# First two products from x times gain, the norm applied to their results, first weight chunks loaded between the quarters of x

## What is computed

```python
def first_block(x, ...):
    for i in range(DEPTH):
        h = _rmsnorm(x, attn_norm[i])
        proj = jnp.matmul(h, w_in[i])
        q_a, c_kv, q_idx, k_idx, w_idx, qkv_b, gate_a, gate_b = _split_cols(proj)
        c_kv = _rmsnorm(c_kv, kv_norm[i])
        ...
        x = x + jnp.matmul(merged, w_out[i])
        ...
```

## Time and profile before

| | us |
|---|---|
| median of 3 runs | 2364.31 |
| lowest, highest | 2362.16, 2365.21 |
| span of the profiled execution | 2358.2 |
| TensorE busy in it | 2261.0 (96%) |
| VectorE, ScalarE, GpSimd busy | 919.8, 772.5, 773.1 |

### The profile page before, as it was taken

The page is one execution under the profiler, slowest core; times in us unless marked ns, Lnnn a source line. Parts: engine busy times, 40 slices in busy tenths (PEclk is TensorE's granted clock), DMA queues, the critical chain, the costliest instruction groups (busy, mean ns, idle before and its releaser), DMA issues.

```text
span 2358.2 us, 30460 instructions
## 1 busy us (share of the span) xinstructions
PE 2261.0 (96%) x12044; PEld 1719.9 (73%) x12044; DVE 919.8 (39%) x1370; ACT 772.5 (33%) x1154; POOL 773.1 (33%) x414
## 2 busy tenths in 40 slices
PE   7999999979999899999999999999999999999997
PEld 5776667633333379668899999888877686888885
DVE  2586453331111463433660362353000524721722
ACT  4335555211111433653421222333322424222222
POOL 3341226211111134204244444334433044544541
PEclk9899999979999999999999999999999999999999
DMA  4421113668999322102223232222322022333330
GB/s 160 144 83 61 45 46 116 245 240 352 353 350 383 115 86 90 45 9 63 65 95 92 89 89 90 90 91 91 96 72 80 1 90 79 98 93 97 98 98 36
DMA packets 69360, 278.03 MB, mean 118 GB/s; under 512 B 13016, under 2 KB 13144, under 8 KB 56960
## 3 DMA queue, kind: packets, MB, share of 16 engines
q1 hardware_dynamic: 59408, 259.61, 31.9%
q0 software_dynamic: 9552, 16.51, 2.0%
q10 hardware_dynamic: 288, 0.34, 0.1%
HBM read 323.58 MB, written 19.42 MB: 145 GB/s over the span
## 4 chain that ended last, share of the span: by engine, by line
PE 87%; DVE 4%; issue 4%; POOL 2%; ACT 2%; DMA 0%; DVEq 0%; POOLq 0%; SPq 0%; ACTq 0%
PE ps L871 19%; PE ps L890 17%; PE ps L1334 7%; PE ps L1093 5%; PE ps L522 4%; PE ps L1136 4%; PE ps L1356 4%; POOL weights_low L2705 2%; PE ps L1295 2%; PE ps L1120 2%; PE ps L641 2%; PE ps L1197 2%; PE ps L732 1%; PE ps L852 1%; PE ps L624 1%
## 5 line engine op out<-in xcount | busy, mean ns | idle before, releaser
L2705 POOL TENSOR_TENSOR weights_low<-weights,parts 128x1024 fp32r<-128x1024 f32 x250 | 632.3, 2534 | 1064.9 <-ACT parts L1884 1064.9
L871 PE MATMUL ps<-parts 128*128 128x264 f32 x2384 | 447.2, 283 | 0.0
L890 PE MATMUL ps<-parts 128*128 128x512 f32 x1344 | 416.1, 390 | 1.3 <-ACT area L1406 1.0
L1884 ACT ACTIVATE parts<-weights 128x1024 fp32r<-128x1024 f32 x257 | 269.1, 1054 | 400.7 <-PE ps L871 133.8
L871 PEld LDWEIGHTS ps<-parts 128*128 128x128 f32 x2384 | 372.9, 188 | 0.0
L871 PE MATMUL ps<-parts,weights_low 128*128 128x264 f32 x1120 | 317.3, 283 | 0.0
L890 PEld LDWEIGHTS ps<-parts 128*128 128x128 f32 x1344 | 252.3, 188 | 56.0 <-issue 1.2
L890 PE MATMUL ps<-parts,weights_low 128*128 128x512 f32 x672 | 262.5, 391 | 0.0
L871 PEld LDWEIGHTS ps<-parts,weights_low 128*128 128x128 f32 x1120 | 211.1, 188 | 0.0
L1334 PE MATMUL ps<-area,normed 128*64 128x512 f32 x752 | 171.5, 597 | 1.6 <-DVE normed L2393 1.6
L2178 DVE TENSOR_TENSOR parts<-normed,parts 128x528 f32 (+1 forms) x64 | 160.5, 2508 | 9.6 <-DVE normed L2177 2.0
(11 more groups left out here) (459 smaller groups left out, 3600.0 us busy)
## 6 DMA issues: line engine op xcount, KB each, us to landing
weights<-in_weights SPq DMA_DIRECT2D x283, 512.0 KB, 3.5
area<-in_experts SPq DMA_DIRECT2D x141, 1024.0 KB
area<-pair_rows SPq DMA_DIRECT2D x4, 1024.0 KB, 7.9
bias_scratch<-bias_vector POOLq DMA_DIRECT2D x1, 2560.0 KB, 18.3
residual<-in_x SPq DMA_DIRECT2D x4, 512.0 KB, 6.4
area<-bias_scratch POOLq DMA_DIRECT2D x1, 2048.0 KB, 9.0
token_rows<-area SPq DMA_DIRECT2D x1, 2048.0 KB, 8.2
out_tiles<-residual SPq DMA_DIRECT2D x4, 512.0 KB, 2.8
```

What stands on the lines that cost most here:

```text
L871: ins = mm(ps[:, b + h, 0:HALF], wt[:, k], x[m * DT + k][:, HALF * h:HALF * h + HALF], start=m == k == j == 0, stop=m == chunks - 1 and k ...
L890: ins = mm(ps[:, b], wt[:, k], x[:, m * DT + k, first:first + SEQ], start=m == k == j == 0, stop=m == chunks - 1 and k == DT - 1 and j == 2)
L1884: fn(high_slot(n, place), RING[:, n % SLOTS], ACT.Copy).then_inc(S["w_hi"], 1)
L2705: g.tensor_tensor(RING_LOW[:, n % SLOTS], RING[:, n % SLOTS], high_slot(n, place), ALU.subtract).then_inc(S["w_lo"], 1)
```

## The change

SyncE issues one quarter of x, chunks 0 and 1, the other three quarters, then chunks 2 to 7. VectorE multiplies each tile of x by its gain alone (`XG`), and TensorE takes the first two products from `XG` and chunks 0 and 1; VectorE multiplies the two results by `R` later. The partition sum of the norm stands behind 13 of those 16 products in TensorE's order. The first two split chunks go through `first_pair`, which waits for a tile of `x_hi` or `x_lo` at a time. Four places instead of two hold high parts of weights, so `high` runs two chunks further ahead, and `high(2)` and `high(3)` stand before and behind the inverse deviation. Squares go to a place of their own (`SQ_FIRST`). The rest of the diff is counts and names.

```diff
-        IN_FIRST = [[part(20480 + D * j, D) for j in range(2)], None]
+        IN_FIRST = [[part(at, D) for at in (20480, 21504, 22528, 32256)], None]
+        XG, SQ_FIRST = area(7168, DT, SEQ), area(23552, DT, SEQ)
...
-            for j in range(4):
+            def load_x(j):
                 sp.dma_start(XA[:, 2 * j:2 * j + 2], a["x"][:, 2 * j:2 * j + 2]).then_inc(x_in[j], 16)
+
+            load_x(0)
...
             for c in range(SLOTS):
                 load(c, slice(c, c + 1))
+                if c == 1:
+                    for j in (1, 2, 3):
+                        load_x(j)
...
                 pe.wait_ge(S["consts"], 32)
-                rms_sum(HA[:, DT - 1])
-
-                hn = lambda k: HA[:, k]
                 begin_stage("act_evac")
+                banks, pair = [bank(), bank()], [take(), take()]
+                for c, k in [(c, k) for k in range(DT - 2) for c in range(2)] + [(c, k) for c in range(2) for k in (DT - 2, DT - 1)]:
+                    if c == 0:
+                        pe.wait_ge(S["norm_out"], w.next("norm_out"))
+                    if (c, k) == (0, DT - 1):
+                        rms_sum(SQ_FIRST[:, DT - 1])
+                    ins = mm(ps[:, banks[c]], pair[c][:, k], XG[:, k], start=k == 0, stop=k == DT - 1)
+                    if (c, k) in ((0, 0), (1, DT - 2)):
+                        begun(ins)
+                    if k == DT - 1:
+                        ins.then_inc(S["tile_done"], 1)
+                first_pair(HH, HL, IN_FIRST, [(0, 0, SEQ)], banks=[bank(), bank()])
                 for n in range(2):
-                    linear(hn, take(), fresh=n == 0)
-                pe.wait_ge(S["x_hi"], w.next("x_hi", DT))
-                pe.wait_ge(S["x_lo"], w.next("x_lo", DT))
-                for n in range(4):
                     linear_split(HH, HL, IN_FIRST)
+                pe.wait_ge(S["norm_out"], w.next("norm_out", DT))
...
-                    fn(HA[:, t], XA[:, t], ACT.Square).then_inc(S["norm_sq"], 1)
+                    fn(SQ_FIRST[:, t], XA[:, t], ACT.Square).then_inc(S["norm_sq"], 1)
                 act.wait_ge(S["consts"], 32)
+                high(2, place=IN_FIRST, slots=-1)
                 inverse_deviation(SEQ, D, "eps1")
+                high(3, place=IN_FIRST, slots=-1)
...
-                for n in (2, 3):
+                for n in (4, 5):
                     high(n, place=IN_FIRST, slots=-1)
...
             def body():
+                dve.wait_ge(S["consts"], 32)
                 for n in range(DT):
-                    total(n, HA, SEQ, "norm_sq", n + 1)
-                dve.wait_ge(S["consts"], 32)
+                    if n % 2 == 0:
+                        dve.wait_ge(x_in[n // 2], 16)
+                    v.tensor_scalar(XG[:, n], XA[:, n], vec("attn_norm", n), None, ALU.mult).then_inc(S["norm_out"], 1)
+                    if n % 2:
+                        for m in (n - 1, n):
+                            total(m, SQ_FIRST, SEQ, "norm_sq", m + 1)
                 rms(8, SEQ, "attn_norm", lambda t: XA[:, t], lambda t: HA[:, t])
                 for t in range(DT):
                     dve.wait_ge(S["x_hi"], w.next("x_hi"))
                     v.tensor_tensor(HL[:, t], HA[:, t], HH[:, t], ALU.subtract).then_inc(S["x_lo"], 1)
+                dve.wait_ge(S["act_evac"], w.next("act_evac", 2))
+                for x in (CKV, KI):
+                    v.tensor_tensor(x, x, R[:, 0:SEQ], ALU.mult).then_inc(S["norm_out"], 1)
```

More of the change, by code:

```diff
@@ L331, in square @@
             return (HA if v < 2 else RK[:, :, B1])[:, 2 * i + v % 2]
[L333 to L336, removed]
+        names = """consts norm_sq norm_sum norm_sd norm_out act_ops dve_ops pool_ops
+            tile_done act_evac dve_evac chunk_begun rel_done rel_sb rel_used score_cut score_mask
+            bias_vec bias_dram bias_rows bias_rep small_in logits smax expd diag tr pt o_done o_evac             z_done soft sp sp_masked c_done a_raw a_masked merged
             route_done route_ev route_e rank_done table_in table_rows table iota_in gate_on sg
@@ L340, in build @@
             p_in meta_in out_done ln_cent ln_out c2_in c3_in hot_in bvec_out wr_in route_x lam_exp gelu_in gelu_th
-            gelu_done xq w_hi w_lo x_hi x_lo lru_t pad_zero lru_x lru_r lru_done hidden mla_ones q_ready k_rope k_ready m_rows m_in mla_s mla_p mla_o mla_om mla_d mla_dm mla_y mla_ym ret_s ret_used ret_o ret_y decay_in sum_part sq_pair hl_kept g_lo roped y_hi y_lo route_t route_c sq_added""".split()
+            gelu_done w_hi w_lo x_hi x_lo lru_t pad_zero lru_x lru_r lru_done mla_ones q_ready k_rope k_ready m_rows m_in mla_s mla_p mla_o mla_om mla_d mla_dm mla_y mla_ym ret_s ret_used ret_o ret_y decay_in sum_part sq_pair hl_kept g_lo roped y_hi y_lo route_t route_c sq_added""".split()
         S = {n: ctx.enter_context(nc.semaphore(n)) for n in names}
@@ L573, in body @@
                         pe.wait_ge(S["bias_dram"], w.next("bias_dram", 1))
+                        pe.wait_ge(S["norm_out"], w.next("norm_out", 2))
                     relevance(range(EACH * c, min(EACH * c + EACH, len(RELS))))
@@ L894, in linear_parts, with first_pair @@
                 ins.then_inc(S["tile_done"], 1)
-            def first_pair(high, low, place, cols):
-                banks = [2 * bank() for _ in range(2)]
+            def first_pair(high, low, place, cols, banks=None):
+                banks = banks or [2 * bank() for _ in range(2)]
                 pair = [take_parts(place) for _ in range(2)]
@@ L1431, in body @@
                     if n >= 2:
-                        high(n + 2, place=IN_FIRST, slots=-1)
+                        high(n + 4, place=IN_FIRST, slots=-1)
                 if w.counted("tile_done"):
@@ L1435, in body @@
                 w.count("tile_done")
+                act.wait_ge(S["norm_out"], w.next("norm_out", 2))
                 squares(1, lambda t: CKV, lambda t: R1)
@@ L1442, in body @@
                     evac(out, bank(n), scale=QK_SCALE if n < 8 else 1.0)
-                    high(n + 8, place=IN_FIRST, slots=-1)
+                    high(n + 10, place=IN_FIRST, slots=-1)
                     for m in range(EACH * n, min(EACH * n + EACH, len(RELS))):
@@ L1452, in body @@
                     fn(HL_KEPT[:, t], HL[:, t], ACT.Copy).then_inc(S["hl_kept"], 1)
-                for n in (20, 21):
-                    high(n, place=IN_FIRST)
                 for n in range(2):
@@ L2030, in body @@
                     chosen_keys(t)
-                dve.wait_ge(S["act_evac"], w.next("act_evac", 30))
+                dve.wait_ge(S["act_evac"], w.next("act_evac", 28))
                 w.count("tile_done", 30 - 6)
@@ L2656, in body @@
                     low(n, IN_PLE)
-                pool.wait_ge(S["norm_out"], w.next("norm_out", 33))
+                pool.wait_ge(S["norm_out"], w.next("norm_out", 43))
                 pool.dma_start(MASKW, a["causal"]).then_inc(S["c2_in"], 16)
```

1 line of the change is left out of this document (added).

## The result

| | before | after |
|---|---|---|
| median of 5 runs, us | 2362.82 (2362.16 to 2365.21) | 2374.09 (2368.73 to 2376.04) |
| ratio | | 1.0041, 95% interval 1.0029 to 1.0053 |
| profiled execution, span in us | 2358.2 | 2371.9 |
| mean granted clock of TensorE | 0.983 | 0.975 |

The forecast was a gain of 2.5 us and the time 2361.8. The change cost 11.3 us by the medians (0.48%; the ratio in the table is taken over all runs and comes out a little lower), more than the upper end of the range (2371.5) left room for.

The account below looks back on a forecast made before the run. TensorE, busy 96% of the span, was taken as the bound. First stage: 29.3 + 21.8 + 0.2 + 1.7 = 53.0 against 55.48 us, so 2364.3 - 2.5 = 2361.8 us; range 2359.5 to 2371.5.

Parts of the forecast that it names:

- Loads and start of the products: First stage: the second chunk takes a quarter of x's place and lands near 8.8 us, where TensorE starts.
- The norm 8.4 us late: First stage: partition sum behind 13 of 16 products ends at 24.0, so normed tiles start at 25.55 against 17.12 us.
- The 13.4 us of products gone from behind the norm: First stage: TensorE products moved ahead of the norm, counted as what the late norm buys.
- Who gets in at 26.6: First stage: GpSimd's low(3) enters between VectorE's normed tiles near 26.9, ends at 29.25; first split product at 29.3; chance 0.54.
- The first two rivals: First stage, low(3): GpSimd waits for VectorE's whole row (6.8 us slower, 0.25) or until normed tiles end (1.9 slower, 0.13).
- the third: First stage loads: chunks land with the rest of x, near 11.4 us; no change (0.1 us slower); chance 0.08.
- the first rival: First stage: GpSimd waits for VectorE's whole row, low(3) at 38.1, stage end 62.3, 6.8 us slower; chance 0.25.
- The sum of the stage: First stage end: 29.3 + 21.8 + 0.2 + 1.7 = 53.0 against 55.48 us, a gain of 2.5 us.
- the clock's fall that it charged: First stage: TensorE stands 2.7 us, from 26.6 to 29.3, and loses its full clock; 1.7 us charged.
- Behind 55 us everything hangs on TensorE as before: Rest of the kernel after the first stage: no cost foreseen there from the change.
- The range: Whole kernel, eight times in ten: 2359.5 to 2371.5 us, taking in most of the rival where GpSimd waits for VectorE's row.
- My 4.3 us with ends of 3.8 and 6.8: First stage: TensorE's cold start at 1.2 GHz lasts 4.3 us, with 2.1 us lost; ends 3.8 and 6.8.

Follow-up runs that it names:

- the four kernels with the late step and no extra products: Changed kernel 2374.09; it with empty instructions 2375.37; it with three added products at 53 us 2377.59; kernel before with ten one-element VectorE writes 2377.76 us.
- the one with three late products: Changed kernel plus three 128x512 float32 products at 53 us that nobody reads, giving back the 2.4 us: 2377.59 us, ratio 1.0061.
- those with ten or twelve writes: One-element VectorE writes at the program's head: ten in the kernel before, 2377.76 us (1.0060); twelve in the changed kernel, 2360.50 us (0.9986).
- the extra products: 14 unread 128x128 products, two behind each head's first tile in the score stage; in the changed kernel 2361.61 us, ratio 0.9990.
- the kernel before with the extra products: Kernel before plus 14 unread 128x128 products in the score stage: 2362.99 us, ratio 0.9993; with ten one-element VectorE writes as well, 2364.29 us.
- all six kernels that had them: With 14 unread score-stage products: changed 2361.61, before 2362.99, before with ten writes 2364.29, changed with earlier partition sum 2357.85, earlier high copies 2357.60, both 2356.33 us.
- the run with the early sum: Changed kernel with 14 unread score-stage products and the partition sum two pairs of products earlier in TensorE's order: 2357.85 us, ratio 0.9977.
- the three of the last group: Changed kernel with 14 unread score-stage products, plus earlier partition sum 2357.85 us, earlier high copies of chunks 3 and 4 2357.60 us, or both 2356.33 us.

## Why the prediction was wrong

**Loads and start of the products**: right. The second chunk landed at 9.2 us (8.8 foreseen), TensorE began at 9.45 (8.8).

**The norm 8.4 us late**: right. Partition sum done at 24.3 (24.0), normed tiles from 25.74 (25.55). TensorE began 0.65 us later than foreseen and took 0.3 less to the sum. The 13.4 us of products gone from behind the norm are 13.1 by the prediction's own rows (15.67 less 2.6); nothing else used them.

**Who gets in at 26.6**: right, and by the rows chosen for it. GpSimd's `low(3)` and VectorE's normed tiles:

```profile
26.74 2.62 POOL L2727 TENSOR_TENSOR weights_low<-weights,parts 128x1024 fp32r<-128x1024 f32 x1 [8.51 <-ACT parts L1898]
34.91 11.30 POOL L2727 TENSOR_TENSOR weights_low<-weights,parts 128x1024 fp32r<-128x1024 f32 x3 [5.56 <-ACT parts L1898]
```

```profile
25.74 7.47 DVE L1951 SCALAR_TENSOR_TENSOR normed<-residual,vectors,rstd 128x512 f32<-128x512 f32 x8 [6.96 <-ACT rstd L1414]
```

The tiles took 7.47 us in place of 5.39: one of them waited for GpSimd, as in the earlier trace rows. The first two rivals, by which GpSimd would have had to wait, didn't occur here, and neither did the third. The next piece, from 34.91, came into the row of subtractions and did wait for its end, as in the earlier trace rows, and beyond it for the products of CKV and KI by `rstd`, which I had put at no cost: they ran from 37.95 to 39.23, and GpSimd's piece ended at 41.5. In this kernel that was free, since TensorE came to it at 42.20. By this row, the first rival's sum had the same 1.2 us too little.

**The sum of the stage**: 53.0 foreseen, 53.08 measured, with the clock's fall that it charged (TensorE stood from 26.8 to 29.45; the granted clock is 0.63 from 29 to 33 us).

**"Behind 55 us everything hangs on TensorE as before"**: this step failed. It put everything behind 55 us at nothing, and there the runs showed 13.5 us lost in the score stage and 2.6 near 2000 us. It was true of who waits for whom, and it left out two things. The change lengthens VectorE's program, so everything behind stands elsewhere in it; and TensorE's speed behind 55 us isn't a constant: in the score stage a third of a microsecond was enough to lower it. The profile of before had a sign of the second: the windows of 990 to 1010 us show TensorE busy for 7.96 and 7.86 of 10 us at a clock of 1.00, while 2.45 us of standing had cost the clock in the first stage. I had read that row as a stage without a problem. It was no proof of danger either: in the kernel before, TensorE is busy for 6.86 us in 10 from 1984.3 to 1994.3, still less, and the clock is 1.00 there. Once the clock had fallen it stayed down for 30 us, through the rest of the scores (the last ends at 1016.6) and 9 us of the next products, in which TensorE didn't wait. VectorE was busy for 4.31 us in 10 in place of 7.46 meanwhile; that their taking turns kept the clock down is a reading that no run tests.

The Trainium skill (TensorE: Matmul & The Clock Gate, "A second HAM failure mode: psum-queue depth-cycling") describes a kernel in which frequent short idle times between groups of products make the clock swing between its two levels. The trace has the short idle times (TensorE waits for VectorE nine times for the scores from 990 us on in the kernel before, 0.8 us at the longest) but not the swinging: no fall in these windows before the change, and one of 30.7 us after it.

**The range** was built from rivals that all lay in the first stage. A cost downstream had no term, though the medians of the four kernels with the late step and no extra products (2374 to 2378 us) lie above it. None of its rivals is what made the kernel slower.

**Still open.** The smaller fall near 2000 us (2.6 us) is in the changed kernel, in the one with three late products and in those with ten or twelve writes; with the extra products it is gone in most and shorter in two. One of these two is the kernel before with the extra products, whose VectorE program is that of before, so a moved fetch of VectorE's is not needed for it. TensorE stands there for over 2 us in the kernel before as well (busy for 0.00 us from 1987 to 1989), at 1.00. No run was aimed at it. That the late step is the wait for the fetched block is inferred from the transfer's moving with it, from "issue" as its releaser and from the ten and twelve writes; the transfer itself shows about 0.6 us behind the start of the late instruction, so behind the end of the wait, and it may be the fetch ahead of the next block that one sees.

## What to carry to other kernels

Look for the stages in which TensorE is at full clock although it waits for another engine turn by turn. In one such stage a delay of 0.34 us cost 13.5 us here, and an edit far ahead that adds ten instructions to another engine's program was enough to bring it. A few products that nobody reads, put into a wait that is there anyway, kept the clock in this stage in all six kernels that had them; 14 of them cost nothing that could be measured. And when a small change shows a loss, compare where both traces stand at several points of time before judging the edit itself: this one did what it should have done and was charged for an accident a thousand microseconds on.

## What the runs showed of the hardware

- An instruction of VectorE can start 0.34 us late with nothing in the profile to wait for. Where this falls moves with the number of instructions ahead of it in the program: it is at the twentieth score tile with ten more instructions than before, and gone from that stage's busy steps with 22 more. The Trainium skill (Runtime: NRT & Kernel Launch, "Instruction fetch mechanics") has it that the sequencer drives its own DMA queue to fetch the next page of instructions while it executes the current one, and that the cost of going from one block to the next is mostly hidden. The trace shows such transfers on a queue of instructions, of 8192 bytes each; at this place 0.34 us wasn't hidden.
- GpSimd got in between two of VectorE's products by `rstd` (2.62 us for its piece) and not between gapless subtractions (6.58 us in the run with the early sum, for one that takes 2.34 to 2.5 alone). What decides is open. It isn't whether there was a gap, since all these rows are gapless, and by the rows it isn't products by `rstd` against subtractions either: in the earlier trace rows GpSimd got in between steps of the same form as the two products of CKV and KI (`area<-area,rstd`, 128x512), and between these it didn't.
- The cold start of TensorE is not one number: from its first product on a record took about 0.85 us, and then 0.43, and it stayed at the first price for 3.5 us in the changed kernel and for 5.5 to 6 us in the three of the last group, by the starts of the L550 records (the column of the granted clock reads 1.00 from 10 us on in the changed kernel and in that with the early sum). My 4.3 us with ends of 3.8 and 6.8 missed the first by a little and covers the others.
- The empty instructions that waited for nothing weren't in the program that ran (30460 instructions with 14 of them and without). Count the instructions on the page before reading such a run.
